# Norm statistics four steps behind their sums, spaced scale diagonals, another tile order in the first FFN round, and earlier SiLU tiles

## The reference, cut to what matters

```python
for l in range(2):
    h = rms_norm(x, norm1_g[l]);  z = h @ w_in[l]
    ya = conformer_conv(z[..., :768], ...)      # GLU, causal conv of width 31, LayerNorm, SiLU, w_pw
    yb = spatial_gating(z[..., 768:1536], ...)  # GELU, LayerNorm(v), causal 128x128 mixing, u * (.)
    yc = multiscale_pool(z[..., 1536:], ...)    # trailing means over 2/4/8/16 positions
    x = x + concat(ya, yb, yc) @ w_out[l]
    h = rms_norm(x, norm2_g[l])
    gate, up = split(h @ w_gate_up[l])          # 2 x 2816 columns
    x = x + (silu(gate) * up) @ w_down[l]
return rms_norm(x, final_g)
```

## Time and profile before

| | |
|---|---|
| runs, median of 3 | 2924.85 us (2922.9 to 2927.22) |
| profiled execution, its own time | 2920.39 us |
| its span, core 1 (granted TensorE clock 0.983) | 2918.8 us |
| spans of the cores | 2903.2 to 2918.8 us |
| PE busy | 2770.4 us, 95% |
| DVE busy | 1222.0 us, 42% |
| ACT busy | 766.0 us, 26% |
| POOL busy | 173.6 us, 6% |
| chain that ended last | PE 87%, DVE 4%, issue 3%, ACT 2%, DMA 2% |

### The profile page before, as it was taken

One profiled execution on the slowest core, in us unless ns is written; L12 is line 12 of the kernel. 1 busy time (PEld: TensorE's weight loads), 2 busy tenths in 40 slices (PEclk: granted clock), 3 DMA queues, 4 the chain that ended last, 5 costly groups with the idle time before them and its releaser, 6 DMA issues.

```text
span 2918.8 us, 42424 instructions; the slowest of 8 cores (2903.2 to 2918.8 us)
## 1 busy us (share of the span) xinstructions
PE 2770.4 (95%) x14844; PEld 1410.5 (48%) x14844; DVE 1222.0 (42%) x2225; ACT 766.0 (26%) x1316; POOL 173.6 (6%) x274
## 2 busy tenths in 40 slices
PE   6998999999999899999979989999999989999997
PEld 4663444444565344444556634444445644444444
DVE  4645232233563432323655462332344643323236
ACT  4553101102544211010354431011035532010112
POOL 2110100000010100000000001000000100000000
PEclk9999999999999999999999999999999999999999
DMA  9321722200313162111342307212003022221102
GB/s 196 58 49 22 103 44 36 37 15 16 58 29 70 25 93 50 36 31 22 141 122 50 50 2 118 37 30 51 15 2 59 23 50 37 34 46 37 37 15 116
DMA packets 124031, 150.35 MB, mean 52 GB/s; under 512 B 71728, under 2 KB 98224, under 8 KB 121776
## 3 DMA queue, kind: packets, MB, share of 16 engines
q0 software_dynamic: 36512, 97.33, 20.0%
q1 hardware_dynamic: 87312, 50.31, 6.3%
HBM read 215.05 MB, written 25.69 MB: 82 GB/s over the span
## 4 chain that ended last, share of the span: by engine, by line
PE 87%; DVE 4%; issue 3%; ACT 2%; DMA 2%; POOL 1%; SPq 1%; DVEq 0%; ACTq 0%; POOLq 0%
PE quad L345 79%; PE quad L363 3%; PE quad L992 3%; PE quad L822 2%; DVE sqr L384 1%; DVE xT L384 1%; ACT sqa L374 1%; DVE h2T L396 1%; DMA xst<-x 1%; PE quad L816 1%; ACT dF L374 1%; POOL r L658 1%; PE quad L644 1%; SPq L337 1%; DMA sgB<-sg_ln_g 0%
## 5 line engine op out<-in xcount | busy, mean ns | idle before, releaser
L345 PE MATMUL quad<-h2T,ring 128*128 128x512 bf16 x5632 | 1225.1, 380 | 0.0
L345 PEld LDWEIGHTS quad<-h2T,ring 128*128 128x128 bf16 x5632 | 550.9, 98 | 668.2 <-issue 11.4
L384 DVE TENSOR_TENSOR act<-tsil,quad 128x512 bf16<-128x512 f32 x352 | 242.0, 687 | 936.2 <-PE quad L345 928.6
L345 PE MATMUL quad<-act,wd 128*128 128x512 bf16 x2816 | 619.7, 379 | 0.1
L374 ACT ACTIVATE tsil<-quad 128x512 f32<-128x512 f32 x352 | 210.1, 597 | 1478.0 <-PE quad L345 1474.9
L384 DVE TENSOR_TENSOR xT<-xT,quad 128x512 f32<-128x512 f32 x640 | 439.0, 687 | 344.2 <-PE quad L345 314.1
L345 PEld LDWEIGHTS quad<-act,wd 128*128 128x128 bf16 x2816 | 273.0, 98 | 321.2 <-issue 2.4
L374 ACT ACTIVATE sqa<-xT 128x512 bf16<-128x512 f32 x320 | 183.4, 619 | 194.0 <-DVE sqr L384 159.6
L345 PE MATMUL quad<-w_a_sb,xb 128*128 128x384 bf16 x1024 | 182.5, 335 | 0.3 <-issue 0.3
L345 PE MATMUL quad<-w_uv_sb,xb 128*128 128x384 bf16 x1024 | 171.0, 326 | 0.0
L345 PEld LDWEIGHTS quad<-w_a_sb,xb 128*128 128x128 bf16 x1024 | 99.3, 99 | 64.8 <-issue 7.4
(11 more groups left out here) (120 smaller groups left out, 1689.9 us busy)
## 6 DMA issues: line engine op xcount, KB each, us to landing
ring<-w_gate_up POOLq DMA_DIRECT2D x88, 512.0 KB, 7.2
wd<-w_down POOLq DMA_DIRECT2D x12, 1536.0 KB, 11.7
xst<-x SPq DMA_DIRECT2D x24, 512.0 KB, 6.8
out<-osF SPq DMA_DIRECT2D x16, 512.0 KB, 2.7
w_a_sb<-w_a POOLq DMA_DIRECT2D x8, 768.0 KB, 21.8
w_uv_sb<-w_uv POOLq DMA_DIRECT2D x8, 768.0 KB, 34.0
yd<-ytok SPq DMA_DIRECT2D x16, 384.0 KB, 2.6
y<-yd SPq DMA_DIRECT2D x128, 48.0 KB, 2.8
```

The source lines that it names most:

```text
L345: ins = e.matmul(out, l, r, start=(first and i == 0), stop=(last and i == n - 1))
L384: return P.add(eng, lambda e, out=out, in0=in0, in1=in1, op=op: e.tensor_tensor(out=out, in0=in0, in1=in1, op=op), reads=reads, writes=writes)
```

## The change

Six edits, of which none changes what is computed.

- A norm has 14 steps. The additions stay at steps 3, 5, 7, 9; the statistics go to 7, 9, 11, 13 and `fin` to 13. There are three `sqr` tiles, taken in turn over all norms.
- In `norm2`, `hq` gets two empty places (the first with the condition), `dia`, three empty places, `bc` and the eight `sc`: 15 places.
- The first FFN chunk takes blocks 0 and 1 for tiles 0, 1, 2, blocks 2 and 3 for tiles 0, 1, 2, then blocks 0 to 3 for tile 3, and the last two block by block. A slot is reloaded when its pair has had 8 items; `after` comes behind item 16.
- `sgB` is loaded before the last `A` instead of behind it, once that tile's norm has been queued.
- The first SiLU tile, `lnt(s, l, 0)`, goes from behind `Z(3)` to between `U(3)` and `ZB(2)`, with the last of the conv LayerNorm work forced out before it.
- The second, `lnt(s, l, 1)`, goes from behind `PT(2)` to between `Z(3)` and `TR(3)`.

```diff
-    sqr = [alloc("sqr%d" % i, [128, NT], BF16) for i in range(2)]
+    sqr = [alloc("sqr%d" % i, [128, NT], BF16) for i in range(3)]
...
         def step(i):
-            if i >= 5 and i % 2 == 1:
-                stat((i - 5) // 2)
+            if i >= 7 and i % 2 == 1:
+                stat((i - 7) // 2)
...
-            if i == 11:
+            if i == 13:
                 fin()
-        for i in range(12):
-            push(lambda i=i: step(i), (kind, s, l, j) if i == 11 else None, nq if kind == "r2" else None)
+        for i in range(14):
+            push(lambda i=i: step(i), (kind, s, l, j) if i == 13 else None, nq if kind == "r2" else None)
...
-        hq.append((dia, None, ("r2", s, l, j)))
+        hq.append((lambda: None, None, ("r2", s, l, j)))
         hq.append((lambda: None, None, None))
+        hq.append((dia, None, None))
+        for _ in range(3):
+            hq.append((lambda: None, None, None))
         hq.append((bc, None, None))
...
             if ci == 0:
-                order = [(fi, j) for j in range(NJ) for fi in range(2)]
-                order += [(fi, j) for fi in range(2, nf) for j in range(NJ)]
+                order = [(2 * h + fi, j) for h in range(2) for j in range(NJ - 1) for fi in range(2)]
+                order += [(fi, NJ - 1) for fi in range(4)]
+                order += [(fi, j) for fi in range(4, nf) for j in range(NJ)]
...
-                if (oi + 1) % 8 == 0 and fp + NRING < NF // 2:
+                uses[fp] = uses.get(fp, 0) + 1
+                if uses[fp] == 2 * NJ and fp + NRING < NF // 2:
                     load_ring(l, fp + NRING, slot)
-                if ci == 0 and oi == 7:
+                if ci == 0 and oi == 15:
                     after()
...
-            A(s, l, 3)
+            need(("r1", s, l, 3))
             dma("sync", sgB[:, 0, :], sg_ln_g_d[l].partition_broadcast(128), [], [sgB.b(0, grp="sgB")])
             dma("sync", sgB[:, 1, :], sg_ln_b_d[l].partition_broadcast(128), [], [sgB.b(1, grp="sgB")])
+            A(s, l, 3)
...
+                    if j + 1 == NJ:
+                        pace[1], pace[2] = 1, 1
+                        lnt(s, l, 0)
                     ZB(s, l, j - 1)
...
-                    pace[1], pace[2] = 1, 1
-                    lnt(s, l, 0)
+                    lnt(s, l, 1)
                 TR(s, l, j)
                 if j > 0:
                     PT(s, l, j - 1)
-            lnt(s, l, 1)
             ZB(s, l, NJ - 1)
             lnt(s, l, 2)
```

More of the change, by code:

```diff
@@ L619, in build_program @@
     sq_rr = [0]
+    sm_rr = [0]
     def norm_closures(s, l, j, rt, kind, with_xb, xbv=False):
@@ L623, in norm_closures @@
         sqs = {}
+        sms = {}
         br = B("r", kind, j)
@@ L633, in add @@
             a, b = sqs[2 * p], sqs[2 * p + 1]
-            tt(sqr[p % 2][:], sqa[a][:], sqa[b][:], ALU.add, [sqa[a].b(), sqa[b].b()], [B("sqr", p % 2)])
+            i = sm_rr[0] % len(sqr)
+            sm_rr[0] += 1
+            sms[p] = i
+            tt(sqr[i][:], sqa[a][:], sqa[b][:], ALU.add, [sqa[a].b(), sqa[b].b()], [B("sqr", i)])
         def stat(p):
@@ L639, in stat, with fn @@
             bk, bb = st["bk"], st["bb"]
-            def fn(e, bk=bk, p=p):
+            i = sms[p]
+            def fn(e, bk=bk, p=p, i=i):
                 ins = None
                 for q in range(4):
-                    ins = e.matmul(bk[:, q:q + 1], sqr[p % 2][:, q * 128:(q + 1) * 128], ocS[:, 0:1],
+                    ins = e.matmul(bk[:, q:q + 1], sqr[i][:, q * 128:(q + 1) * 128], ocS[:, 0:1],
                                    start=(p == 0 and q == 0), stop=(p == 3), skip_group_check=True)
                 return ins
-            P.add("tensor", fn, reads=[B("sqr", p % 2), bC], writes=[bb])
+            P.add("tensor", fn, reads=[B("sqr", i), bC], writes=[bb])
         def mkxb(k):
@@ L1051, in FFN @@
         cnt = [0]
+        uses = {}
         for ci, (f0, nf) in enumerate(CHUNKS):
```

## The result

The changed kernel takes 2846.57 us (median of 2845.88, 2846.57 and 2848.73; a fourth execution took 3202.63 at a clock of 0.86 on cores 4 to 7, and such disturbed ones, which came with every kernel, are left out of all that follows) against 2924.85 of the kernel before beside it. Their ratio is 0.9734, with a 95% interval of 0.9711 to 0.9756. The profiled execution took 2845.88 us where that of before took 2920.39, 74.5 us less; its span is 2844.3 us on core 5, at a mean granted clock of 0.987, and the cores lie between 2836.9 and 2844.3 us. The forecast was 2845.

A forecast was written before the change was run, and what follows sets the result against it. PE, busy 95% of the span, was taken as the bound, so only its idle time and half-speed stretches could be won. The terms summed to -80 us, giving 2845 us on the median, range 2818 to 2882 (8 in 10).

The forecast's parts named there:

- T1: Theory after the result, the prediction's own: terms are separate, parts made alone add up, conv waits for its DMA chain.
- T2: Theory after the result: the gain is the emptied diagonals' alone, and the other parts move waits about.
- T3: Theory after the result: the order of the first FFN round, put at nothing by the prediction, carries part of the gain.
- Diagonals: `WO` and FFN start: with `bc` later behind `fin`, PE's waits and the half speed behind them go; -39 us.
- Tile 2: FFN start: PE waits 2.5 us, four times, for this tile's last `sc`, plus half speed; +13 us, bounds 0 and +26.
- Statistics: All norms: two more steps between addition and matmul cut PE's waits; -5.5, -6.5, -3, -8 and -3 us by stage.
- SiLU tiles: Around `ZB(2)` to `TR(3)`: moved tiles end the transposes' wait and half speed, new wait for `xc`; -20 us, bounds -10, -24.
- `sgB` early: Before the last `A`: `y` loads land faster without `sgB` beside them, conv starts sooner; -8 us, bounds 0 and -17.
- Order of the first FFN round: First FFN chunk: moves no work, and `w_down`, issued behind item 16, has 27.7 us to land; cost 0.
- (a): Rival: stalls change their name, PE waits for banks or statistics later, half speed stays in conv; 2884 us, chance 0.27.
- (b): Rival: the clock follows, all half-speed stretches go and tile 2 costs nothing; 2805 us, chance 0.12.
- (c): Rival: `w_down` lands late at the end of the first chunk in three layers; 2942 us at 60 us landing, chance 0.02.

The follow-up runs named there:

- the diagonals' kernel: Kernel before with the spaced diagonals and the new tile order alone, norms kept at 12 steps: 2880.35 us, ratio 0.9795.

## Why the prediction was right, by its steps

The parts made alone give -58 (norm, diagonals, order), -21 (SiLU) and 0 (`sgB`) against the medians of before, together -79, where the whole gave -78. In the profiled executions they give -53, -17 and +1, together -69, where the whole gave -74.5. So T1 holds in its main point, that the parts add up within some 6 us, and T2 falls: SiLU alone is a quarter. T3 holds too, as told below.

- *Diagonals*, reckoned at -39: 42 to 45 us in the run of their own. 35.1 us of wait fell to 1.1. Of the rest, half speed is one part: in the four FFN stretches the mean clocks lose 10.7 us before and 5.1 here. No run divides what is left. Right in mechanism, and 3 to 6 us too small.
- *Tile 2*, reckoned at +13: 9.0 us of wait and one group in four at half speed, 1.7 us, make +11. The size and the mechanism are right (a run of its own shows that it hangs on the longer norm).
- *Statistics*, reckoned at -26: waits fell by 15.3 us for `sqr`, and the 2.7 us for `sqa` left the list. Adding the 14 steps to the diagonals' kernel gave 8 us in the profiled executions and 14 in the medians; with the 11 us of tile 2, which came with them, that is -19 to -25. `WO` and the FFN's start came to zero and the start of the kernel to 10.7, as reckoned. Between the sequences 24.6 us of wait became 18.0: 6.6 saved, where 8 were reckoned, 2 of these for half speed. **Mis-sized** are two terms. The ends of the first layers keep 2.5 of 3.5 us of wait each, 2 saved, where 6.5 were reckoned: that two steps of PE's work exceed the longest wait of 1.3 did not empty it, since the longest wait there is still 1.36 us, and with two more steps of delay 2.0 us each are left. In the last stretch 12.1 became 11.4 (3 reckoned). There the step "freed from waiting for PE it gains about 1 us a tile" failed, and two more steps leave 9.9.
- *SiLU tiles*, reckoned at -20: 17 to 21. The new wait for `xc` was named; it came in sequence 0 (1.6 us twice) and not in sequence 1. One reading is off: the sum puts 0.13 us between the transposes and the table load, and the rows show 0.58 (190.33 + 1.91 = 192.24, the load at 192.82). The SiLUs are thus ready 4.65 us behind the transposes and not 4.2, still ahead of the 5.0 at which PE comes, and `SP(3)` didn't wait.
- *`sgB` early*, reckoned at -8: nothing. **The step that failed** is "SP has it issued before the last store of `ytok`, which comes some 10 us later". SP's queue is in order, and ahead of `sgB` it has the eight `y` loads of tile 2, 4.5 us of issue that begin only when that tile's store has landed. So `sgB` goes out at 87.22, 2.84 us and not 10 before the store, takes 5.2 to 6.4 us to land in the first three layers, and lengthens the store by 2.5 us, which is the conv chain's first link. With `sgB` from POOL's queue both the store's 2.6 us and the conv wait of about 6 that the prediction named are there (6.6). The time from `V(0)`'s first matmul to conv's was 12.79, 13.86, 12.82 and 13.30 us before in the four layers, and 14.22, 13.88, 13.73 and 11.66 in the changed kernel. In this queue I looked only at what stands behind the moved load, and not at what stands ahead of it. The 4 us for conv at full speed fell with it; conv's blocks at half speed even rose from 15 to 20 of 48, but with `sgB` early alone they were 9, so that this number says little.
- *Order of the first FFN round*, reckoned at 0: right as to `w_down`, which landed 17.1 us behind its issue and made nobody wait. But 0 for "it moves no work" hides what it does. Without it the same change is 33 us slower, and the longer norm alone is probably a loss. The prediction had tile 3 as never late because it took the new order as given; its worth is that it holds off a loss of the other parts.

Of the rivals, (a), the stalls that change their name, happened at two places: conv (its whole term) and the last stretch (nearly all of it). (b), all half speed gone, did not come: the mean clock rose to 0.987, where 0.990 was forecast, and conv ran at full speed throughout only when its chain was covered. (c), `w_down` late, did not occur. Of the signs named, the statistics (45.0 us for 38) and conv's wait (11.3 for 6) missed too; those for `dF`, `silT`, `xc`, `h2T` and DVE's wait for `sgB` held. The chances of "faster" add up to 0.96 by the prediction's own rule, where it says 0.95.

That 2846.57 lies so close to 2845 is in part luck, since errors cancel: 8 us too much for `sgB` and 1 to 7 for the statistics, against 3 to 6 too little for the diagonals and 2 for tile 2. The profiled execution was to take 2840 by the sum and took 2845.88; the 4.5 us added for the median (0.7 in this kernel) hid most of that. The mechanisms of the diagonals, of tile 2 and of the SiLU tiles are not luck: each was seen in a run of its own or in its own wait.

## What to carry to other kernels

When side work is made to come later, list for each of its consumers how much PE work stands before it, and reorder the main work so that the latest consumer comes last; the reordering is costless only because of this, and without it the delay can turn from gain to loss. When a load is moved ahead on an in-order queue, look at what stands ahead of it in its new place and what waits to land beside it; another queue can be worth more than another place. A chain of a store and loads that can't be shortened (here a store of 5 us and 7 us of loads) can be covered by moving independent matmuls in front of its consumer: that gave 18 to 20 us for one line, half of it from the clock.

## What the runs showed of the hardware

- Half speed doesn't need a long wait just before it. In the fourth layer of the changed kernel conv waits 1.10 us, its first block runs at full speed and the third at half. With `sgB` on POOL a wait of 1.84 us in the first layer was followed by full speed throughout, and waits of 1.46 to 1.66 in the other three by half speed from the second or third block on. What decides between the two I didn't find.

```profile
2193.47 0.37 PE L823 MATMUL quad<-cb,onesb 32*128 32x512 bf16 x1 [1.10 <-issue]
2193.78 1.00 PE L829 MATMUL quad<-toep,y 128*128 128x128 bf16 x12
...
2196.73 1.50 PE L829 MATMUL quad<-toep,y 128*128 128x128 bf16 x12
```

- A store that moves beside two loads spread over all partitions took 5.1 us instead of 2.6, with `V(1)` ahead of conv 6.9 and with statistics six steps behind 7.3, in the first layer each. Where the loads had under 1 us left to go when it was issued, it took 2.6 (`sgB` early alone, third layer: loads issued at 1550.89 and 1551.36 that landed in 3.3 to 3.4 us, store at 1554.09).
